# Weight products that stream their columns from last to first

## The chip, the cores and the metric
One NeuronCore of one Trainium2 chip. The metric is device time in microseconds (us) of one execution; the kernel before takes 2789.39 us, the median of three runs (2787.94 to 2789.61).

## The reference
Two transformer blocks over 256 positions of width 2048, in float32. The first block is a mixer (pooling and a gated delta rule), cross attention over a memory of 256 positions, and a gated feed-forward with a convolution of three taps. The second has a modulation computed from a vector, an attention with several branches, and a feed-forward with squared ReLU. Most of the work is products of 256 rows with large weight matrices:

```
h @ w_in   [2048, 5136]        h @ w_gate, h @ w_up   [2048, 5632]
y @ w_mix_out [2048, 2048]     f @ w_down             [5632, 2048]
h @ w_xq, mem_h @ w_xkv, o @ w_xo                     2048 x (2048, 4096, 2048)
second block: w_in_2 [2048, 5656], w_o_2 [2048, 2048], w_up_2 [2048, 8192], w_down_2 [8192, 2048]
```

## The kernel before
Every weight product is a `Phase`: n iterations over nb column blocks of `width` columns (512, in the first product 428, in the phase w_in2a 432), each block over `units` units of four K-tiles of 128 rows. Weights are float32 and the products are made with three matmuls each in the type float32r: the activations are split into a high and a low part beforehand (hhi and hlo, bhi and blo, fhi and flo, mhi and mlo, f2hi and f2lo), and the weights on the way. For each product of a K-tile, a column block and a half of the positions (128 of the 256, `h`), TensorE adds high x high, high x low and low x high into the same PSUM bank.

A unit's path is this. SyncE issues a transfer of 1 MB (856 or 864 KB in the narrow phases) from HBM into one of four `raw` slots (L817). ScalarE rounds two K-tiles at a time to float32r into `whi` (L1468), VectorE subtracts that from the raw values into `wlo` (L1960). `whi` and `wlo` are rings of four tiles of 128 x 2 x 512. TensorE waits on `unit_used` for a pair of tiles, runs twelve matmuls over it (two K-tiles, two halves, three parts; L1006 to L1008) and increments `mm_done`, for which ScalarE waits before it overwrites that place of the ring. A `raw` slot is free for the next transfer when VectorE has read it.

The weights are the moving operand (128 x width), the activations the stationary one (128 x 128). The result of a block lies in the PSUM tile `GP`, four banks of 512 float32 columns: banks 0 and 1 for the even block, 2 and 3 for the odd one. When the last K-tile has been added, ScalarE or VectorE reads the bank in the ordinary order. `last_units` (L965 to L979) holds the same three matmuls (L975 to L977) for the last two units of the last block of the last product, sorted by half. Between the products TensorE also transposes activations (L959) and computes the small matrices of the attention parts; these are plain float32 matmuls and transposes that the change does not touch (L401, L1149, L1153, L1375, L1425 among them).

The order of the work on each engine is written out by hand, and semaphores tie the engines together.

Of the kernel before, what the change touches and what calls it, by code (L numbers as in the profile page):

```python
# [31 lines left out]
UK = 4  # L32
# [114 lines left out]
def program(nc, A, out):  # L147
    PH = plan()
    order = list(PH.values())
    with ExitStack() as ctx:  # L150
        sems = {}

        def S(name):
            if name not in sems:
                sems[name] = ctx.enter_context(nc.semaphore(name))
            return sems[name]
# [8 lines left out]
        whi = [nc.alloc_sbuf_tensor_at(f"whi{i}", [P, 2, 512], F32R, offset=ring0 + 4096 * i) for i in range(NRING)]  # L165
        wlo = [nc.alloc_sbuf_tensor_at(f"wlo{i}", [P, 2, 512], F32R, offset=ring0 + 4096 * (NRING + i)) for i in range(NRING)]
# [49 lines left out]
        GP = ctx.enter_context(nc.psum_tensor("GP", [P, 4, 512], F32))  # L216
# [740 lines left out]
        def _(pe):  # L957
# [3 lines left out]
            def product(q, ahi, alo, ready, mid=None, end=None, first=None, points={}, halves=None):  # L961

                def last_units(it, b):  # L965
                    for h in range(NH):
                        t = slice(h * P, h * P + P)
                        o = GP[:, 2 * b + h, 0:q.width]
                        for u in (q.units - 2, q.units - 1):
                            for s in range(2):  # L970
                                pe.wait_ge(S("unit_used"), it * (2 * len(q.seq)) + 2 * (q.unit0 + q.seq.index(("g", b, u))) + s + 1 + CREDIT)
                                r = (q.rank[b, u] * 2 + s) % NRING
                                for k in range(2):
                                    kt = u * UK + 2 * s + k
                                    pe.matmul(o, ahi[:, kt, t], whi[r][:, k, 0:q.width], start=False, stop=False)  # L975
                                    pe.matmul(o, ahi[:, kt, t], wlo[r][:, k, 0:q.width], start=False, stop=False)
                                    m = pe.matmul(o, alo[:, kt, t], whi[r][:, k, 0:q.width], start=False, stop=(kt == q.units * UK - 1))  # L977
                                if h:
                                    m.then_inc(S("mm_done"), 1)  # L979
                        if h == 0:  # L980
                            m.then_inc(S("half_mm"), 1)

                def iteration(it, late):
                    for b, u in q.rank:
                        if q.name == "down23" and isinstance(it, int) and it == q.n - 1 and b == q.nb - 1 and u >= q.units - 2:
                            if u == q.units - 1:
                                last_units(it, b)
                            continue
                        if u == 0:
                            pe.wait_ge(S(f"evac{b % 2}"), it * (q.nb // 2) + (q.ev0 + b // 2 + 1))  # L990
                        if b == 0 and not halves:
                            pe.wait_ge(*ready(u))
                        for s in range(2):
                            if b == 0 and halves:
                                pe.wait_ge(*halves(u, s))
                            pos = q.seq.index(("g", b, u))

                            pe.wait_ge(S("unit_used"), it * (2 * len(q.seq)) + 2 * (q.unit0 + pos) + s + 1 + CREDIT)
                            r = (q.rank[b, u] * 2 + s) % NRING
                            for k in range(2):  # L1000
                                kt = u * UK + 2 * s + k
                                first, last = kt == 0, kt == q.units * UK - 1
                                for h in range(NH):
                                    t = slice(h * P, h * P + P)
                                    o = GP[:, 2 * (b % 2) + h, 0:q.width]
                                    pe.matmul(o, ahi[:, kt, t], whi[r][:, k, 0:q.width], start=first, stop=False)  # L1006
                                    pe.matmul(o, ahi[:, kt, t], wlo[r][:, k, 0:q.width], start=False, stop=False)  # L1007
                                    m = pe.matmul(o, alo[:, kt, t], whi[r][:, k, 0:q.width], start=False, stop=last)  # L1008
                            m.then_inc(S("mm_done"), 1)
                        if mid and b % 2 == 1 and u == 1:  # L1010
                            mid(it)
                        if late and b == 0 and u == 0:
                            late()
                        if (b, u) in points:
                            points[b, u]()
                        if isinstance(it, int) and (it, b, u) in points:
                            points[it, b, u]()
                    if q.ada:

                        pe.wait_ge(S("unit_used"), it * (2 * len(q.seq)) + 2 * (q.unit0 + len(q.seq)) + CREDIT)  # L1020
                        pe.wait_ge(S("ada_read"), it + (q.ada0 + 1))
                        if q.name == "ffn1a":
                            pe.wait_ge(S("f1_f"), it + 1)
                        for j in range(4):
                            m = turn(TB[:, 512 + j * P:512 + (j + 1) * P], ada_acc[:, j * P:(j + 1) * P])
                        m.then_inc(S("ada_sum"), 1)

                if end or first:
                    iteration(0, first)
                    if q.n > 1:  # L1030
                        with loop(pe, q.n - 1) as i:
                            iteration(i + 1, (lambda: end(i)) if end else None)
                    return (lambda: end(q.n - 1)) if end else None
                with loop(pe, q.n) as it:
                    iteration(it, None)
# [23 lines left out]
            def unit_of(v):  # L1059
                return v // 8, v % 8 // 4, v % 4  # L1060
# [76 lines left out]
            for hf in range(NH):  # L1137
                for j, m_ in enumerate(("upto", "after", "chunk0", "chunk1")):
                    m = pe.matmul(GP[:, 0, 32 * hf + 8 * j:32 * hf + 8 * j + 8], C(m_), gdec[:, hf * 8:hf * 8 + 8], start=True, stop=True)
                m.then_inc(S("dn_sum"), 1)  # L1140
            for hf in range(NH):
# [6 lines left out]
                for b in range(2):  # L1148
                    pe.matmul(B8[:, 4 * b:4 * b + 4, :].rearrange("p a b -> p (a b)"), C("ones"),  # L1149
                              KB[:, 4 * b:4 * b + 4, :].rearrange("p a b -> p (a b)"),  # L1150
                              start=True, stop=False, skip_group_check=True)
                    for h in range(4 * b, 4 * b + 4):
                        m = pe.matmul(B8[:, h, :], KB[:, h, :], C("negones"), start=False, stop=(h % 4 == 3),  # L1153
                                      skip_group_check=True)
                m.then_inc(S("dn_diff"), 1)
            for hf in range(NH):
                pe.wait_ge(*((S("dn_ex"), 2) if hf else (S("cv_e"), 6)))
                pe.wait_ge(S("dn_kb"), hf + 1)
                for h in range(8):
                    m = turn(AB[hf][0][:, h, :], hd(hf, 1)[:, h, :])  # L1160
                m.then_inc(S("dn_t"), 1)
            for hf in range(NH):
                pe.wait_ge(S("dn_dm"), hf + 1)
                for h in range(8):
                    m = turn(AB[hf][1][:, h, :], DN[hf]["KB"][:, h, :])
                m.then_inc(S("dn_t"), 1)
            for hf in range(NH):
                pe.wait_ge(S("dn_tc"), hf + 1)
                pe.wait_ge(S("dn_qn"), hf + 1)
                for h in range(8):  # L1170
                    m = turn(AB[hf][0][:, h, :], hd(hf, 0)[:, h, :])
                m.then_inc(S("dn_t"), 1)
            for hf in range(NH):
                pe.wait_ge(S("dn_tc"), hf + 3)
                for h in range(8):
                    m = pe.matmul(AB[hf][1][:, h, :], DN[hf]["KT"][:, h, :], DN[hf]["KBT"][:, h, :], start=True, stop=True)
                m.then_inc(S("dn_lt_mm"), 1)
            for hf in range(NH):
                pe.wait_ge(S("dn_tc"), hf + 5)
                for h in range(8):  # L1180
                    m = pe.matmul(AB[hf][0][:, h, :], DN[hf]["KT"][:, h, :], DN[hf]["QT"][:, h, :], start=True, stop=True)
                m.then_inc(S("dn_at_mm"), 1)
            for hf in range(NH):
                pe.wait_ge(S("dn_lt"), hf + 1)
                pe.wait_ge(S("dn_qd"), hf + 1)
                for h in range(8):
                    m = turn(AB[hf][1][:, h, :], hd(hf, 0)[:, h, :])
                m.then_inc(S("dn_t"), 1)
            for hf in range(NH):
                pe.wait_ge(S("dn_tc"), hf + 7)  # L1190
                for e in range(2):
                    pe.wait_ge(S("lv_m"), 2 * hf + e + 1)
                    for h in range(4 * e, 4 * e + 4):
                        m = turn(AB[hf][1][:, h, :], DN[hf]["MT"][:, h, :])
# [29 lines left out]
            for hf in range(NH):  # L1224
# [3 lines left out]
                for h in range(8):  # L1228
                    m = pe.matmul(AB[hf][0][:, h, :], DN[hf]["AA"][:, h, :], hd(hf, 2)[:, h, :], start=True, stop=True)
                m.then_inc(S("dn_uu"), 1)  # L1230
                for h in range(8):
                    m = pe.matmul(AB[hf][1][:, h, :], DN[hf]["KB"][:, h, :], DN[hf]["AA"][:, h, :], start=True, stop=True)
                m.then_inc(S("dn_uw"), 1)
            pe.wait_ge(S("dn_kd"), 2)
            for n in range(4):
                hf, c = divmod(n, 2)
                r = slice(64 * c, 64 * c + 64)
# [6 lines left out]
                if n:  # L1244
                    for e in range(2):
                        pe.wait_ge(S(f"sc_u{e}"), n)
                        for h in range(4 * e, 4 * e + 4):
                            m = pe.matmul(both[:, h, :], WQ[:, h, :], ST[:, h, :], start=(h % 4 == 0), stop=False, skip_group_check=True)
                        m.then_inc(S(f"sc_w{e}"), 1)
                for e in range(2):  # L1250
                    if n:
                        pe.wait_ge(S(f"sc_v{e}"), n)
                    if n < 3:
                        if n == 1 and e == 0:
                            pe.wait_ge(S("dn_oc"), 1)
                        for h in range(4 * e, 4 * e + 4):
                            m = pe.matmul(other[:, h, :], k3[r, h, :], V[r, h, :], start=True, stop=True)
                        m.then_inc(S(f"sc_s{e}"), 1)
                for h in range(8):
                    m = pe.matmul(both[r2, h, :], DT[r, h, r], V[r, h, :], start=(n == 0), stop=True, skip_group_check=True)  # L1260
                m.then_inc(S("sc_o"), 1)

            def dn_turn():
                for hf in range(NH):
# [3 lines left out]
                    for h in range(8):  # L1268
# [6 lines left out]
                    first=lambda: None, points={(0, 0, 1): dn_turn} | {((6 + k) // 8, *list(PH["mix_out"].rank)[(6 + k) % 8]): lambda k=k: raw_turn(1, k)  # L1275
                                                                       for k in range(8)})
            product(PH["xkva"], mhi, mlo, lambda u: (S("norm_lo"), 8 + 2 * u + 2))
            product(PH["xkvb"], mhi, mlo, lambda u: (S("norm_lo"), 16),
                    first=lambda: None, points={unit_of(2 * k): lambda k=k: raw_turn(2, k) for k in range(8)})
# [10 lines left out]
            def query_turn(g):  # L1290
# [7 lines left out]
                for f in range(4):  # L1298
# [6 lines left out]
                    first=lambda: pe.wait_ge(S("norm_lo"), 24), points={unit_of(k): lambda k=k: key_turn(k) for k in range(4)} |  # L1305
# [1232 lines left out]
```

## Time and profile before

| | |
|---|---|
| median of three runs | 2789.39 us |
| profiled execution, first to last instruction (span) | 2785.1 us |
| time around the span (median less span) | 4.3 us |
| TensorE matmuls under way | 2725.2 us, 98%, 13302 instructions |
| TensorE weight loads | 2329.5 us, 84% |
| VectorE busy | 1772.1 us, 64% |
| ScalarE busy | 1324.0 us, 48% |
| GpSimd busy | 169.5 us, 6% |
| moved by DMA | 579.60 MB, mean 208 GB/s |

The profile gives the span of the profiled execution and no time outside it, so what lies around the span is taken from the median. A matmul's duration runs from its start to the end of its pipeline, and several overlap; the distance from one start to the next tells how much of the engine one takes. Idle time of an engine is put down to the instruction that released it.

### The profile page before, as it was taken

Reading aid. Unit: us, or ns where it says so; the run is one execution under the profiler, and the core shown is the slowest. Engines: PE = TensorE matmul, PEld = TensorE weight load, DVE = VectorE, ACT = ScalarE, POOL = GpSimd, SP = SyncE. Lnnn points to the kernel's source line nnn. Section 1 sums busy time; section 2 is a strip of 40 time slices with the busy share of each in tenths; the row PEclk is TensorE's granted clock in tenths of the full one; section 3 lists DMA queues with packets and bytes.
Section 4 is the critical chain, followed back from the end, with each engine's and each line's share of the span. In section 5 each row is a group of like instructions: output and inputs, shape, how many; then the busy total and the mean of one; then the engine's idle time right before and its main releaser. Section 6 shows DMA issues by size and latency. Waiting matters only on the chain.

```text
span 2785.1 us, 34787 instructions
## 1 busy us (share of the span) xinstructions
PE 2725.2 (98%) x13302; PEld 2329.5 (84%) x13302; DVE 1772.1 (64%) x2025; ACT 1324.0 (48%) x1679; POOL 169.5 (6%) x132
## 2 busy tenths in 40 slices
PE   8999999999999999999999999998989999999998
PEld 8999988888888888888888799887868888888887
DVE  4477488776578888765555564547775756645455
ACT  5555444454445454434455454446455344344443
POOL 0001620000000000000000002720000000000000
PEclk9999999999999999999999999999999999999999
DMA  8554068887477777775555556640755866755553
GB/s 284 164 170 131 1 242 275 290 278 261 164 259 273 273 279 272 274 257 182 194 182 200 181 188 204 200 151 1 259 180 197 280 204 238 261 189 177 191 185 132
DMA packets 293266, 579.60 MB, mean 208 GB/s; under 512 B 9168, under 2 KB 46192, under 8 KB 292112
## 3 DMA queue, kind: packets, MB, share of 16 engines
q1 hardware_dynamic: 291296, 566.08, 60.4%
q0 software_dynamic: 1120, 8.57, 0.8%
q10 hardware_dynamic: 720, 3.15, 0.3%
q8 instruction: 90, 1.47, 0.2%
q14 instruction: 40, 0.33, 0.0%
HBM read 575.66 MB, written 2.10 MB: 207 GB/s over the span
## 4 chain that ended last, share of the span: by engine, by line
PE 95%; DVE 3%; ACT 1%; issue 1%; DMA 0%; SPq 0%; POOL 0%; DVEq 0%; ACTq 0%
PE GP L1006 28%; PE GP L1008 28%; PE GP L1007 28%; PE TA L959 2%; PE TB L959 2%; PE TB L607 1%; PE TB L426 1%; PE GP L401 0%; PE TA L1375 0%; DVE wlo L1960 0%; PE GP L1216 0%; PE TA L1216 0%; PE GP L1203 0%; DMA x<-in_x 0%; DVE x L2402 0%
## 5 line engine op out<-in xcount | busy, mean ns | idle before, releaser
L1960 DVE TENSOR_TENSOR wlo<-raw,whi 128x1024 fp32r<-128x1024 f32 (+2 forms) x904 | 1088.2, 1217 | 812.2 <-ACT whi L1468 803.2
L1468 ACT CAST whi<-raw 128x1024 fp32r<-128x1024 f32 (+2 forms) x904 | 923.7, 1029 | 1170.8 <-PE GP L1008 1109.5
L1006 PE MATMUL GP<-whi,hhi 128*128 128x512 f32 (+2 forms) x1792 | 689.9, 385 | 1.9 <-issue 1.4
L1008 PE MATMUL GP<-whi,hlo 128*128 128x512 f32 (+2 forms) x1792 | 681.6, 380 | 0.0
L1007 PE MATMUL GP<-wlo,hhi 128*128 128x512 f32 (+2 forms) x1792 | 680.8, 380 | 0.0
L1006 PEld LDWEIGHTS GP<-whi,hhi 128*128 128x128 f32 x1792 | 338.1, 189 | 52.2 <-issue 3.3
L1008 PEld LDWEIGHTS GP<-whi,hlo 128*128 128x128 f32 x1792 | 337.8, 188 | 52.0
L1007 PEld LDWEIGHTS GP<-wlo,hhi 128*128 128x128 f32 x1792 | 338.3, 189 | 50.5 <-issue 1.0
L1006 PE MATMUL GP<-whi,bhi 128*128 128x512 f32 x704 | 277.0, 393 | 0.2 <-DVE blo L2021 0.2
L1948 DVE SCALAR_TENSOR_TENSOR ada_acc<-raw,csig,ada_acc 128x512 f32<-128x512 f32 x360 | 270.3, 751 | 10.2
L1008 PE MATMUL GP<-whi,blo 128*128 128x512 f32 x704 | 274.6, 390 | 0.0
L1007 PE MATMUL GP<-wlo,bhi 128*128 128x512 f32 x704 | 274.3, 390 | 0.0
L1006 PE MATMUL GP<-whi,f2hi 128*128 128x512 f32 x496 | 195.4, 394 | 0.0
L1008 PE MATMUL GP<-whi,f2lo 128*128 128x512 f32 x496 | 193.3, 390 | 0.0
L1007 PE MATMUL GP<-wlo,f2hi 128*128 128x512 f32 x496 | 193.3, 390 | 0.0
L1008 PEld LDWEIGHTS GP<-whi,blo 128*128 128x128 f32 x704 | 132.2, 188 | 27.8
L1006 PEld LDWEIGHTS GP<-whi,bhi 128*128 128x128 f32 x704 | 132.3, 188 | 26.9 <-DVE blo L2021 0.7
L1007 PEld LDWEIGHTS GP<-wlo,bhi 128*128 128x128 f32 x704 | 132.4, 188 | 26.5
L1006 PE MATMUL GP<-whi,fhi 128*128 128x512 f32 x352 | 137.5, 391 | 0.0
L1008 PE MATMUL GP<-whi,flo 128*128 128x512 f32 x352 | 137.2, 390 | 0.0
L1007 PE MATMUL GP<-wlo,fhi 128*128 128x512 f32 x352 | 137.1, 390 | 0.0
L1007 PEld LDWEIGHTS GP<-wlo,f2hi 128*128 128x128 f32 x496 | 93.2, 188 | 20.0 <-issue 1.0
(437 smaller groups left out, 2578.2 us busy)
## 6 DMA issues: line engine op xcount, KB each, us to landing
raw<-in_w_up SPq DMA_DIRECT2D x108, 1024.0 KB, 5.4
raw<-in_w_down SPq DMA_DIRECT2D x108, 1024.0 KB, 5.1
raw<-in_w_ada SPq DMA_DIRECT2D x96, 1024.0 KB, 5.2
raw<-in_w_gate SPq DMA_DIRECT2D x44, 1024.0 KB, 5.3
raw<-in_w_in SPq DMA_DIRECT2D x48, 856.0 KB, 4.7
raw<-in_w_xkv SPq DMA_DIRECT2D x32, 1024.0 KB, 5.7
raw<-in_w_in SPq DMA_DIRECT2D x24, 1024.0 KB, 5.0
raw<-in_w_in SPq DMA_DIRECT2D x24, 864.0 KB, 4.7
```

The lines of the kernel that those rows point to most:

```text
L426: m = pe.matmul(TB[:, 512 * (n % 2) + d * P:512 * (n % 2) + d * P + P], kv[:, k, c:c + P], pT[:, k, j, :], start=(k == 0), stop=(k == 1), ...
L607: m = pe.matmul(bank[:, j * P:j * P + P], l, r, start=(d == 0), stop=(d == len(terms) - 1), skip_group_check=True)
L959: return pe.transpose(dst, src, ident[0:n, 0:n] if n != P else ident)
L1006: pe.matmul(o, ahi[:, kt, t], whi[r][:, k, 0:q.width], start=first, stop=False)
L1007: pe.matmul(o, ahi[:, kt, t], wlo[r][:, k, 0:q.width], start=False, stop=False)
L1008: m = pe.matmul(o, alo[:, kt, t], whi[r][:, k, 0:q.width], start=False, stop=last)
L1468: nc.scalar.copy(whi[(2 * g + s) % NRING][:, :, 0:q.width], raw[j % NSLOT][:, 2 * s:2 * s + 2, 0:q.width])\
L1948: m = nc.vector.scalar_tensor_tensor(ada_acc[:, :], raw[j % NSLOT][:, k, :], c, ada_acc[:, :], ALU.mult, ALU.add)
L1960: TTo(wlo[r][:, :, 0:q.width], raw[j % NSLOT][:, 2 * s:2 * s + 2, 0:q.width], whi[r][:, :, 0:q.width].bitcast(F32), ALU.subtract).then_inc ...
```

## The change
In both places where weight products are issued, the moving operand and the output are indexed with `[:, ::-1]` on the column dimension. The moving operand is read from column width-1 down to 0, and the result of its first column is written to the last PSUM column, and so on down. The stationary operand, the contents of all tiles, the flags and all waits and increments stay. Column j of the weights still ends in column j of PSUM.

```diff
@@ last_units
-                        o = GP[:, 2 * b + h, 0:q.width]
+                        o = GP[:, 2 * b + h, 0:q.width][:, ::-1]
...
-                                    pe.matmul(o, ahi[:, kt, t], whi[r][:, k, 0:q.width], start=False, stop=False)
-                                    pe.matmul(o, ahi[:, kt, t], wlo[r][:, k, 0:q.width], start=False, stop=False)
-                                    m = pe.matmul(o, alo[:, kt, t], whi[r][:, k, 0:q.width], start=False, stop=(kt == q.units * UK - 1))
+                                    pe.matmul(o, ahi[:, kt, t], whi[r][:, k, 0:q.width][:, ::-1], start=False, stop=False)
+                                    pe.matmul(o, ahi[:, kt, t], wlo[r][:, k, 0:q.width][:, ::-1], start=False, stop=False)
+                                    m = pe.matmul(o, alo[:, kt, t], whi[r][:, k, 0:q.width][:, ::-1], start=False, stop=(kt == q.units * UK - 1))
@@ iteration
-                                    o = GP[:, 2 * (b % 2) + h, 0:q.width]
-                                    pe.matmul(o, ahi[:, kt, t], whi[r][:, k, 0:q.width], start=first, stop=False)
-                                    pe.matmul(o, ahi[:, kt, t], wlo[r][:, k, 0:q.width], start=False, stop=False)
-                                    m = pe.matmul(o, alo[:, kt, t], whi[r][:, k, 0:q.width], start=False, stop=last)
+                                    o = GP[:, 2 * (b % 2) + h, 0:q.width][:, ::-1]
+                                    pe.matmul(o, ahi[:, kt, t], whi[r][:, k, 0:q.width][:, ::-1], start=first, stop=False)
+                                    pe.matmul(o, ahi[:, kt, t], wlo[r][:, k, 0:q.width][:, ::-1], start=False, stop=False)
+                                    m = pe.matmul(o, alo[:, kt, t], whi[r][:, k, 0:q.width][:, ::-1], start=False, stop=last)
```

## Rows read from the trace of the kernel before

**Rows 1.** The page: engine busy times, and TensorE's granted clock in 40 slices.
```profile
PE 2725.2 (98%) x13302; PEld 2329.5 (84%) x13302; DVE 1772.1 (64%) x2025; ACT 1324.0 (48%) x1679; POOL 169.5 (6%) x132
...
PEclk9999999999999999999999999999999999999999
```

**Rows 2.** The page: the chain that ended last, by engine and by line.
```profile
PE 95%; DVE 3%; ACT 1%; issue 1%; DMA 0%; SPq 0%; POOL 0%; DVEq 0%; ACTq 0%
PE GP L1006 28%; PE GP L1008 28%; PE GP L1007 28%; PE TA L959 2%; PE TB L959 2%; PE TB L607 1%; PE TB L426 1%; PE GP L401 0%; PE TA L1375 0%; DVE wlo L1960 0%; PE GP L1216 0%; PE TA L1216 0%; PE GP L1203 0%; DMA x<-in_x 0%; DVE x L2402 0%
```

**Rows 3.** Waits, longest first: total us, times, longest (all; TensorE's; the transfer queue's).
```profile
ACT whi L1468 <- PE GP L1008: 1109.5, 755, 3.6
DVE wlo L1960 <- ACT whi L1468: 803.2, 607, 4.5
...
PE TA L959 <- DVE xn_p L2303: 11.3, 1, 11.3
...
PE GP L1006 <- DVE wlo L1960: 0.5, 1, 0.5
...
SPq L817 <- DVE wlo L1960: 2097.6, 448, 110.1
```

**Rows 4.** Groups by line and shape, matmuls of L1006 and L975: busy, mean ns | idle.
```profile
L1006 PE MATMUL GP<-whi,hhi 128*128 128x512 f32 x1216 | 481.5, 396 | 1.9 <-issue 1.4 <-DVE wlo L1960 0.5
L1006 PE MATMUL GP<-whi,bhi 128*128 128x512 f32 x704 | 277.0, 393 | 0.2 <-DVE blo L2021 0.2
L1006 PE MATMUL GP<-whi,f2hi 128*128 128x512 f32 x496 | 195.4, 394 | 0.0
L1006 PE MATMUL GP<-whi,hhi 128*128 128x428 f32 x384 | 139.4, 363 | 0.0
L1006 PE MATMUL GP<-whi,fhi 128*128 128x512 f32 x352 | 137.5, 391 | 0.0
L1006 PE MATMUL GP<-whi,mhi 128*128 128x512 f32 x256 | 100.9, 394 | 0.0
L1006 PE MATMUL GP<-whi,hhi 128*128 128x432 f32 x192 | 69.0, 359 | 0.0
L975 PE MATMUL GP<-whi,f2hi 128*128 128x512 f32 x16 | 6.2, 390 | 0.0
```

**Rows 5.** Timeline, three stretches: start us, duration us, engine, line, operation.
```profile
102.32 0.36 PE L1006 MATMUL GP<-whi,hhi 128*128 128x428 f32 x1
102.33 0.19 PEld L1007 LDWEIGHTS GP<-wlo,hhi 128*128 128x128 f32 x1
...
103.50 0.36 PE L1006 MATMUL GP<-whi,hhi 128*128 128x428 f32 x1
...
1500.17 0.39 PE L1007 MATMUL GP<-wlo,fhi 128*128 128x512 f32 x1
...
1505.61 0.39 PE L1007 MATMUL GP<-wlo,fhi 128*128 128x512 f32 x1
...
1689.72 0.36 PE L1006 MATMUL GP<-whi,hhi 128*128 128x432 f32 x1
...
1692.65 0.36 PE L1006 MATMUL GP<-whi,hhi 128*128 128x432 f32 x1
```

**Rows 6.** The chain in order of time (first row), then single lines: durations min/median/max.
```profile
731.76 6.92 PE GP L401 x32
...
L1149 PE MATMUL TB<-flat,cst x4: 593/594/677, 262.4 to 264.6; 128*128 128x512 f32 x4
L1425 PE MATMUL TA<-dg,cst x16: 590/592/697, 1960.2 to 2537.5; 128*128 128x512 f32 x16
L1153 PE MATMUL TB<-cst,flat x16: 272/275/276, 263.3 to 265.8; 128*128 128x128 f32 x16
L1375 PE MATMUL TA<-rc,w1c x128: 191/275/276, 1756.4 to 1831.4; 128*128 128x31 f32 x128
```

## The prediction

> **What bounds the kernel now.** I read the page first: TensorE has matmuls under way in 98% of the span and its granted clock is 9 tenths or more, the upper of its two levels (2.4 GHz), in every one of 40 slices [rows 1]. Busy time of a pipelined engine can mislead, so the chain of waits comes next: of the work that ended last 95% is TensorE's, and the three matmul lines that the change edits, L1006 to L1008, hold 28% each [rows 2]. Third are the waits. ScalarE waited 1109.5 us for L1008 and VectorE waited 803.2 us for ScalarE, that is, the two engines that prepare weight tiles are ahead and stand behind TensorE's release of a ring tile; the transfer queue waited 2097.6 us for VectorE in turn. TensorE's own longest wait is 11.3 us, and for the prepared weights it waited 0.5 us in all [rows 3]. So the pace at which TensorE streams one weight matmul sets the time, and whatever that pace gains or loses is the change's whole effect.
>
> **How many, and how far apart.** Grouped by shape, line 1006 has 1216 + 704 + 496 + 352 + 256 matmuls of 512 columns, 384 of 428 and 192 of 432; L975 has 16 more of 512 columns [rows 4]. L1007 and L1008 (and L976, L977) run once for each of these, so 3 x 3040 = 9120 matmuls have 512 columns, 1152 have 428, 576 have 432; 10848 are touched.
> The mean durations (390 to 396 ns) are not their price, as matmuls overlap. Their spacing is: from 1500.17 to 1505.61 us lie 24 starts, 226.7 ns each, at 512 columns; from 102.32 to 103.50 lie 6, 196.7 ns each, at 428; from 1689.72 to 1692.65 lie 15, 195.3 ns each, at 432 [rows 5]. The sum 9120 x 0.2267 + 1152 x 0.1967 + 576 x 0.1953 = 2067.5 + 226.6 + 112.5 = 2406.6 us is 86% of the span of 2785.1 us, against some 85% in the chain, so the spacing is the right price.
> At 2.4 GHz 512 columns take 213.3 ns at one a cycle. The stream therefore already runs at one column a cycle, with a gap of 13.4 ns per matmul. The narrow ones have 178.3 and 180.0 ns of columns in a spacing 16 to 18 ns longer; their weight loads last 0.19 us [rows 5] and probably hold them, so that a small cost to the narrow matmuls may be partly covered.
>
> **The change part by part.** It adds no instruction, no wait, no byte and no transfer. Tiles, tile order, the semaphores and the ring are untouched. No queue is passed and nothing moves past a wait. Where a matmul writes, only the order within its own bank row changes, and every consumer waits for the whole matmul. Two orders turn round.
> 1. The moving operand is read from its last column to its first. Step is one element (4 bytes) back in place of one forward. All 512 are still neighbours.
> 2. The PSUM columns are written last to first. The consumers read the bank as before.
> No row of the trace has a matmul with a backward operand, so the price has to be bounded. From below: the 13.4 ns gap goes altogether, 9120 x 13.4 ns = 122 us; nothing excludes it, though nothing in the order of columns suggests it. From above: the nearest rows of a slower stream are the plain float32 matmuls. 32 of L401 with 256 columns take 6.92 us, 216 ns each, which is 0.845 ns or two cycles a column [rows 6]; and at equal shape, 128x512, L1149 and L1425 last 594 and 592 ns against 390 ns of the edited lines [rows 4, 6], 203 ns more. If a backward column cost two cycles, spacings would be 432, 361 and 365 ns, so 9120 x 0.206 + 1152 x 0.165 + 576 x 0.170 = 1879 + 190 + 98 = +2167 us.
> I take nothing, zero, of this range for either order. The reason is locality: the backward stream touches the same words of the same row, and words that were neighbours in time still are; only the sign of the step differs. The row that it is nearest to is the same matmul forward, same bytes and same tiles, rather than the float32 matmul, whose operands are another type. Same engine, same clock: L1375's moving slices of 31 floats start at odd offsets for every other l [rows 6] and show a median of 275 ns, no different from the 275 ns of L1153 with 128 aligned columns; but both look bound by the weight load, so this is weak support.
> What would hide a cost: nothing. With the preparers waiting for TensorE [rows 3], each nanosecond on a matmul is 10.8 us on the kernel. What comes late next if TensorE slows: nobody, the others only wait longer. ScalarE's and VectorE's exposure does not change, as PSUM is read in the old order in the other banks.
> A rule of the Trainium skill speaks against the change. Its page "PSUM — Partial Sum Buffer" (Specifications) has PSUM in lines of 8 bytes, two float32 values, and says that any non-contiguous access pattern slows matmuls significantly; the page "SBUF — State Buffer" (section "SBUF: two separate sides") has 16-byte lines in SBUF that give full rate when a line is hit at least twice in a row. No row here has a non-contiguous operand at this width, so neither is tested by the trace. Read as a rule on the step's sign, the first would give the two-cycle rival below; read as a rule on lines, both give nothing: widths 512, 428 and 432 are even and start at column 0, so backward neighbours still share their lines. I hold the second reading the likelier.
>
> **The sum.** 2785.1 us of span + 4.3 us around it (median 2789.4 less the span) + 0 = 2789.4 us, the median of the runs shown.
>
> **Rivals.**
> A, slower by far: one of the two address streams pairs neighbours only when the address rises, and falls to one column each two cycles. Its place is every edited matmul, its price the +2167 us above: 2789 + 2167 = 4956 us. It decides as soon as a column takes more than one cycle. For it: two cycles a column is a pace that this engine shows on other operands [rows 6], and the forward stream runs so near the ceiling that it has no reserve. Against it: neighbours stay neighbours. If a column took more than two cycles it would be above that.
> B, slower a little: a fixed cost at the head of a backward matmul, such as a first fetch that is no longer ready. It spans from the visible 0.5 ns per matmul (5.6 us) to a second gap of 13.4 ns, 9120 x 13.4 = 122 us and 0 to 23 us for the 1728 narrow ones: 2795 to 2935 us, 2861 with half a gap. For it: there is a 13.4 ns gap now, so heads of matmuls are not free. Against it: the addresses are known well ahead of the matmul.
> C, faster: the gap comes from writes of one matmul meeting the next one's at the same end of the bank and the backward order eases it: down to 2667 us with the whole gap. Against it: both matmuls turn round, so their distance in the bank stays what it was.
> D, the reversal of both sides is folded away before it reaches the chip, or the engine treats both signs alike: the time is that of the forecast, and I count it there.
>
> **Chances.** Forecast and D 0.68, A 0.18, B 0.11, C 0.03. A measurement of this kernel can tell some 0.2% (5.6 us) from no change; so faster 0.03, same 0.68, slower 0.29. The range goes from 2783 (0.2% below) to 2936 us, which takes in the forecast, all of B and a little of C, 0.8 in sum, and leaves A out; the forecast's own range is 2784 to 2795.
>
> **What will show it.** Right: start-to-start spacing of L1006 to L1008 at 512 columns stays at 226 to 227 ns, their durations at 390 ns, ScalarE's wait for L1008 at about 1110 us. A shows as a spacing above 400 ns, durations near 590 ns, a ScalarE wait above 3000 us, DMA at half its rate. B shows as the same added nanoseconds on 512 columns whatever the tile, and fewer on 428 and 432. Wrong altogether would be a spacing that differs between L1007 and L1008, whose operands lie in different tiles: then it is the place of data and not the order.

## The result and the profile after

The kernel takes 2844.14 us, the median of four runs (2842.31 to 2846.10), against 2788.66 us before (2786.57 to 2789.61). The ratio is 1.020, 95% interval 1.0187 to 1.0213: slower by 55.5 us. The forecast was no change (2789.4 us). The time lies inside the stated range, in the part that rival B held (2795 to 2935 us). The profiled execution took 2844.97 us, of which 2843.1 us is span.

The page of the kernel after: engine busy times, the granted clock in 40 slices, the chain of waits by engine.
```profile
PE 2785.1 (98%) x13302; PEld 2329.2 (82%) x13302; DVE 1777.2 (63%) x2025; ACT 1323.1 (47%) x1679; POOL 167.7 (6%) x132
...
PEclk9999999999999999999999999999999999999999
...
PE 96%; DVE 2%; ACT 1%; issue 1%; DMA 0%; SPq 0%; POOL 0%; DVEq 0%; ACTq 0%
```
The clock and the kind of bound are as in [rows 1, 2]. TensorE's busy time rose by 59.9 us; the busy times of weight loads, VectorE and ScalarE moved by 5.1 us at most.

Waits of the kernel after, in the columns of [rows 3].
```profile
ACT whi L1468 <- PE GP L1008: 1170.8, 761, 3.6
...
DVE wlo L1960 <- ACT whi L1468: 851.8, 613, 4.7
...
PE TA L959 <- DVE xn_p L2303: 11.3, 1, 11.3
```
No new wait has come. ScalarE stands 61 us longer behind TensorE and VectorE 49 us longer behind ScalarE; that is the delay passed on, not a cause.

The cause is seen in the spacing. Timeline of TensorE after, three stretches as in [rows 5].
```profile
103.32 0.36 PE L1006 MATMUL GP<-whi,hhi 128*128 128x428 f32 x1
...
105.68 0.36 PE L1006 MATMUL GP<-whi,hhi 128*128 128x428 f32 x1
...
1529.72 0.40 PE L1007 MATMUL GP<-wlo,fhi 128*128 128x512 f32 x1
...
1535.32 0.40 PE L1007 MATMUL GP<-wlo,fhi 128*128 128x512 f32 x1
...
1719.87 0.36 PE L1006 MATMUL GP<-whi,hhi 128*128 128x432 f32 x1
...
1723.42 0.36 PE L1006 MATMUL GP<-whi,hhi 128*128 128x432 f32 x1
```
At 512 columns 24 starts take 5.60 us, 233.3 ns each, where it was 226.7 ns: +6.7 ns. At 428 columns 12 starts take 2.36 us, 196.7 ns each, and at 432 columns 18 starts take 3.55 us, 197.2 ns each. Set beside [rows 5], 428 columns seem not to have moved, but the six starts there are too few: printed starts are rounded to 0.01 us, and before the change the spacing at 428 columns differs from stretch to stretch. Longer stretches of the kernel before:
```profile
154.85 0.36 PE L1007 MATMUL GP<-wlo,hhi 128*128 128x428 f32 x1
...
168.38 0.36 PE L1008 MATMUL GP<-whi,hlo 128*128 128x428 f32 x1
...
1615.30 0.36 PE L1007 MATMUL GP<-wlo,hhi 128*128 128x432 f32 x1
...
1723.02 0.36 PE L1008 MATMUL GP<-whi,hlo 128*128 128x432 f32 x1
```
and the same ones after:
```profile
156.87 0.36 PE L1007 MATMUL GP<-wlo,hhi 128*128 128x428 f32 x1
...
170.63 0.37 PE L1008 MATMUL GP<-whi,hlo 128*128 128x428 f32 x1
...
1648.44 0.36 PE L1007 MATMUL GP<-wlo,hhi 128*128 128x432 f32 x1
...
1756.97 0.36 PE L1008 MATMUL GP<-whi,hlo 128*128 128x432 f32 x1
```
The 70 starts at 428 columns take 13.53 us before and 13.76 us after, 193.3 and 196.6 ns each; the 550 starts at 432 columns 107.72 and 108.53 us, 195.9 and 197.3 ns each.

The mean over the whole trace gives the price. It takes every distance below 260 ns from one weight matmul to the next of the same width: 227.1 ns before and 233.4 ns after at 512 columns (+6.3), 195.1 and 196.7 ns at 428, 195.9 and 197.3 ns at 432 (+1.5 each). At 512 columns the even stretches before run at 226.7 ns, but single distances of 231 to 236 ns lie between them, which lifts that mean to 227.1. With the counts of the prediction, 9120 x 6.3 ns + 1728 x 1.5 ns = 57.5 + 2.6 = 60.1 us; the span grew by 2843.1 - 2785.1 = 58.0 us. So the sum explains the whole, and 2 us too much: the some 120 distances of 260 ns and more at 512 columns did not grow but fell by 2.0 us in all.

Groups by line and shape after, in the columns of [rows 4].
```profile
L1006 PE MATMUL GP<-whi,bhi 128*128 128x512 f32 x704 | 282.1, 401 | 0.0
L1007 PE MATMUL GP<-wlo,bhi 128*128 128x512 f32 x704 | 279.9, 398 | 0.0
L1008 PE MATMUL GP<-whi,blo 128*128 128x512 f32 x704 | 279.7, 397 | 0.0
...
L1006 PE MATMUL GP<-whi,hhi 128*128 128x428 f32 x384 | 140.9, 367 | 0.0
```
Durations are 7 to 8 ns longer at 512 columns (401 against 393 ns in the first row). It is the same for the three lines, whose moving tiles differ, so the place of the data has no part in it.

### The profile page after: what moved, and what is told of

Its sections match the earlier page's. It is cut to its first block, busy times and chain, and to the rows that moved or that the text cites. A ratio compares the mean times of both kernels' runs of the same rounds, so it can differ in the third digit from the quotient of the medians.

```text
span 2843.1 us, 34787 instructions
## 1 busy us (share of the span) xinstructions
PE 2785.1 (98%) x13302; PEld 2329.2 (82%) x13302; DVE 1777.2 (63%) x2025; ACT 1323.1 (47%) x1679; POOL 167.7 (6%) x132
## 4 chain that ended last, share of the span: by engine, by line
PE 96%; DVE 2%; ACT 1%; issue 1%; DMA 0%; SPq 0%; POOL 0%; DVEq 0%; ACTq 0%
PE GP L1006 29%; PE GP L1007 29%; PE GP L1008 29%; PE TA L959 2%; PE TB L959 2%; PE TB L607 1%; PE TB L426 1%; PE GP L401 0%; PE TA L1375 0%; PE GP L1203 0%; PE TA L1203 0%; PE GP L1216 0%; PE TA L1216 0%; DMA x<-in_x 0%; DVE wlo L1960 0%
## 5 line engine op out<-in xcount | busy, mean ns | idle before, releaser
L1006 PE MATMUL GP<-whi,hhi 128*128 128x512 f32 (+2 forms) x1792 | 699.8, 390 | 2.0 <-issue 1.4
L1007 PE MATMUL GP<-wlo,hhi 128*128 128x512 f32 (+2 forms) x1792 | 691.8, 386 | 0.0
L1008 PE MATMUL GP<-whi,hlo 128*128 128x512 f32 (+2 forms) x1792 | 691.7, 386 | 0.0
L1006 PEld LDWEIGHTS GP<-whi,hhi 128*128 128x128 f32 x1792 | 337.6, 188 | 61.4 <-issue 3.7
L1008 PEld LDWEIGHTS GP<-whi,hlo 128*128 128x128 f32 x1792 | 337.4, 188 | 60.5
L1007 PEld LDWEIGHTS GP<-wlo,hhi 128*128 128x128 f32 x1792 | 337.7, 188 | 58.1 <-issue 1.0
L1006 PE MATMUL GP<-whi,bhi 128*128 128x512 f32 x704 | 282.1, 401 | 0.0
L1007 PE MATMUL GP<-wlo,bhi 128*128 128x512 f32 x704 | 279.9, 398 | 0.0
L1008 PE MATMUL GP<-whi,blo 128*128 128x512 f32 x704 | 279.7, 397 | 0.0
L1006 PE MATMUL GP<-whi,f2hi 128*128 128x512 f32 x496 | 199.2, 402 | 0.0
L1007 PE MATMUL GP<-wlo,f2hi 128*128 128x512 f32 x496 | 197.1, 397 | 0.0
L1008 PE MATMUL GP<-whi,f2lo 128*128 128x512 f32 x496 | 197.1, 397 | 0.0
L1008 PEld LDWEIGHTS GP<-whi,blo 128*128 128x128 f32 x704 | 132.4, 188 | 31.8
L1006 PEld LDWEIGHTS GP<-whi,bhi 128*128 128x128 f32 x704 | 132.4, 188 | 31.1 <-DVE blo L2021 0.4
L1007 PEld LDWEIGHTS GP<-wlo,bhi 128*128 128x128 f32 x704 | 132.5, 188 | 30.7
L1006 PE MATMUL GP<-whi,fhi 128*128 128x512 f32 x352 | 140.2, 398 | 0.0
L1007 PE MATMUL GP<-wlo,fhi 128*128 128x512 f32 x352 | 139.9, 397 | 0.0
L1008 PE MATMUL GP<-whi,flo 128*128 128x512 f32 x352 | 139.9, 397 | 0.0
L1006 PEld LDWEIGHTS GP<-whi,f2hi 128*128 128x128 f32 x496 | 93.3, 188 | 23.0 <-issue 1.0
```

Source lines behind the costliest of these rows:

```text
L1006: pe.matmul(o, ahi[:, kt, t], whi[r][:, k, 0:q.width][:, ::-1], start=first, stop=False)
L1007: pe.matmul(o, ahi[:, kt, t], wlo[r][:, k, 0:q.width][:, ::-1], start=False, stop=False)
L1008: m = pe.matmul(o, alo[:, kt, t], whi[r][:, k, 0:q.width][:, ::-1], start=False, stop=last)
```

## The experiments

**1 and 2: one stream at a time.** Experiment 1 reverses only the moving operand, experiment 2 only the output.
```diff
# 1: the three moving operands, output as before
+ pe.matmul(o, ahi[:, kt, t], whi[r][:, k, 0:q.width][:, ::-1], ...)
# 2: the output, moving operands as before
+ o = GP[:, 2 * (b % 2) + h, 0:q.width][:, ::-1]
```
Expected of 1: 

> Only the moving operand is read backwards; PSUM is written forwards, so the columns of every weight product come out in reversed order (the computation is changed in that, its amount is not). Theory R (the backward read costs 6.7 ns per matmul of 512 columns): spacing 233.3 ns, time about 2844 us. Theory W (the backward write costs it): spacing 226.7 ns, time about 2789 us. Theory B (each stream has a share, or only the pair costs): in between, for instance 230 ns and 2817 us.

Expected of 2: 

> Only the PSUM columns are written backwards; the moving operand is read forwards, so the columns of every weight product come out in reversed order. Theory R: spacing 226.7 ns, about 2789 us. Theory W: spacing 233.3 ns, about 2844 us. Theory B: in between, about 230 ns and 2817 us.

Measured: reading backwards 2845.68 us, ratio to before 1.0208 (1.0191 to 1.0225); writing backwards 2786.83 us, ratio 0.9998 (0.9988 to 1.0008), beside 2787.59 us of the kernel before in the same session. Timeline of TensorE with the read backwards:
```profile
2305.75 0.40 PE L1008 MATMUL GP<-whi,hlo 128*128 128x512 f32 x1
...
2311.35 0.40 PE L1008 MATMUL GP<-whi,hlo 128*128 128x512 f32 x1
```
and with the write backwards:
```profile
2305.71 0.39 PE L1007 MATMUL GP<-wlo,hhi 128*128 128x512 f32 x1
...
2311.15 0.39 PE L1007 MATMUL GP<-wlo,hhi 128*128 128x512 f32 x1
```
Both pairs are 24 starts apart: 5.60 us or 233.3 ns each, and 5.44 us or 226.7 ns each. The read carries the whole cost, the write none. Over the whole trace the means at 512 columns are 233.4 ns with the read backwards and 227.1 ns with the write backwards, as after and before the change. Theory R stands, W and B fall.

**3 and 4: which part of going backwards.** Experiment 3 takes groups of four columns from last to first and goes forwards inside them; experiment 4 takes the groups forwards and goes backwards inside. Both streams have the pattern.
```diff
# 3, on the output and the three moving operands
+ whi[r][:, k, 0:q.width].rearrange("p (a b) -> p a b", b=4)[:, ::-1, :]
# 4
+ whi[r][:, k, 0:q.width].rearrange("p (a b) -> p a b", b=4)[:, :, ::-1]
```
Expected of 3: 

> Both streams go through groups of four columns (16 bytes) from the last group to the first, and forwards within a group; the result is in place. If the sign of the step across lines costs, spacing 233.3 ns as in the changed kernel. If the sign of the step from word to word costs, 226.7 ns. If the cost came per line and not per matmul, it would show here more than there: 128 groups in each matmul. A two-level pattern may have a price of its own, up to two cycles a column (above 420 ns).

Expected of 4: 

> Both streams go through the groups of four columns forwards, and through the four columns of a group backwards; the result is in place. If the sign of the word-to-word step costs, 233.3 ns or more; if the sign across lines costs, 226.7 ns. As a third way, the pattern starts at column 3 and ends at 508, so the head of the next matmul lies near the start of the row as in the kernel before: if the place of the first column costs, 226.7 ns here and 233.3 ns with groups from last to first.

Measured, one run each: 2849.07 us and 2790.65 us. Timeline of experiment 3:
```profile
2305.62 0.40 PE L1008 MATMUL GP<-whi,hlo 128*128 128x512 f32 x1
...
2311.22 0.40 PE L1008 MATMUL GP<-whi,hlo 128*128 128x512 f32 x1
```
and of experiment 4:
```profile
2305.72 0.39 PE L1007 MATMUL GP<-wlo,hhi 128*128 128x512 f32 x1
...
2311.16 0.39 PE L1007 MATMUL GP<-wlo,hhi 128*128 128x512 f32 x1
```
Again 24 starts each: 233.3 and 226.7 ns. A negative step inside 16 bytes is free, 384 of them per matmul. Going from group to group backwards costs the full 6.7 ns, and the 127 jumps cost no more than 511 single steps do. In experiment 3 both streams have the pattern, so that its cost too is the read's is inferred from experiments 1 and 2, and not shown for groups.

**5: whose cost it is.** Only the second of the three matmuls is reversed.
```diff
+ pe.matmul(o[:, ::-1], ahi[:, kt, t], wlo[r][:, k, 0:q.width][:, ::-1], start=False, stop=False)
```
Expected: 

> Only the second of the three matmuls (L1007, and L976) reads and writes backwards, the result stays in place. Theory H (a fixed cost of each backward matmul): mean spacing (2 x 226.7 + 233.3) / 3 = 228.9 ns, about 2808 us, and the trace shows which spacing is the long one: the one that begins with the start of L1007 if the backward matmul holds the stream longer, the one that ends there if its own start is late. Theory T (the cost comes at a change between matmuls, because a backward one ends at column 0 and the next backward one begins at 511, or because directions differ): all three spacings move, or none.

Measured: 2806.81 us, one run; a third of 55.5 us above before would be 2807. Groups of experiment 5:
```profile
L1007 PE MATMUL GP<-wlo,bhi 128*128 128x512 f32 x704 | 278.8, 396 | 0.0
...
L1008 PE MATMUL GP<-whi,blo 128*128 128x512 f32 x704 | 274.7, 390 | 0.0
```
Between 2230 and 2498 us, in the mean of the distances below 260 ns and from the trace's starts in whole nanoseconds, 232.5 ns lie from L1007 to the next start, 226.7 from L1006 and 227.5 from L1008. Against the 226.7 ns of an even forward stretch the reversed matmul takes 5.8 ns more and the one that follows it 0.8 more, together 6.7 ns before rounding; the one before it does not change. (From the printed starts the same means come out at 233.3, 226.8 and 226.7. Three distances take 686.7 ns here, nine take 2060, so the rounding to 0.01 us falls alike again and again and does not average out.) Nearly all of the cost lies in the distance that begins with the reversed matmul's own start. Theory H stands and T, by which all three would have moved or none, falls.

**6, 11 and 12: how coarse the jumps may be.** Groups of 256, 16 and 64 columns, last group first, forwards inside; in 11 and 12 only the products of 512 columns.
```diff
+ def groups_back(w, n=16):        # 12: n=64; 6: n = width // 2 and no condition
+     return w.rearrange("p (a b) -> p a b", b=n)[:, ::-1, :] if w.shape[1] == 512 else w
```
Expected of 6: 

> Both streams read the upper half of the columns forwards, then the lower half forwards (one jump backwards per matmul, first column 256); the result stays in place. Theory P (the place of the first column, or a single backward jump, costs 6.7 ns): 233.3 ns. Theory L (the cost belongs to stepping backwards from line to line, and 511 steps and 127 jumps of four columns reached the same limit): 226.7 ns, about 2788 us.

Expected of 11: 

> Both streams of the 512-column products go through groups of 16 columns from the last to the first, forwards inside a group; the narrow products are forward. 31 backward jumps per matmul, against 127 with groups of four (233.3 ns) and one with groups of 256 (226.7 ns). Theory count (each backward line step costs a little, up to a ceiling): between, 227 to 233 ns. Theory head (only the first few fetches count, the stall comes when they go backwards): with four lines forward at the head the stall is gone, 226.7 ns. Theory place (a start far from column 0 and near the end of the row costs): 233.3 ns.

Expected of 12: 

> The same with groups of 64 columns: 7 backward jumps, first column 448. Theory count: 226.7 to 228 ns. Theory head: 226.7 ns. Theory place: 233.3 ns, as column 448 is nearer the end of the row than 256, which cost nothing.

Measured, one run each: 2785.73 us with groups of 256, 2847.24 us with 16, 2786.44 us with 64. Timeline with groups of 16:
```profile
2305.66 0.40 PE L1010 MATMUL GP<-wlo,hhi 128*128 128x512 f32 x1
...
2311.26 0.40 PE L1010 MATMUL GP<-wlo,hhi 128*128 128x512 f32 x1
```
and with groups of 64:
```profile
2306.05 0.39 PE L1009 MATMUL GP<-whi,hhi 128*128 128x512 f32 x1
...
2311.49 0.39 PE L1009 MATMUL GP<-whi,hhi 128*128 128x512 f32 x1
```
24 starts each, 233.3 and 226.7 ns; groups of 256 give 226.7 ns too. The cost is all there or not at all: full with 511, 127 and 31 backward jumps, none with 7 and 1. The graded form of theory count falls, as does theory head as I had put it (four groups of 16 bytes at the head would have been enough). A count that tips over between 7 and 31 jumps and a head longer than 16 columns are both left open. So is a third reading that no run separates from these: the step back grows with the group, 1, 7 and 31 columns long where it costs, 127 and 511 where it does not. As in experiment 3, both streams have the pattern. Theory place is dealt with under experiment 10.

**7 and 8: is the weight load in the way?** 64 in place of 128 stationary columns, on all K-tiles but the first and last of a block; 8 reads and writes backwards as well.
```diff
+ np_ = P if first or last else 64
+ t = slice(h * P, h * P + np_)
+ o = GP[0:np_, 2 * (b % 2) + h, 0:q.width]
```
Expected of 7: 

> The kernel before, but for the K-tiles other than the first and the last of a block only 64 of 128 stationary columns are used (half of the output rows are left out there). Theory S (the gap beyond 213.3 ns is the weight load's reads standing in the way of the moving reads, so it goes with the number of stationary columns): gap halves from 13.3 to 6.7 ns, spacing 220 ns. Theory F (the gap is fixed per matmul): 226.7 ns.

Expected of 8: 

> As the kernel with 64 stationary columns, both moving read and PSUM write backwards. Theory S: the gap of 20 ns of the changed kernel halves, spacing 223.3 ns. Theory F: 233.3 ns, or 6.7 ns above the forward kernel of this kind whatever that is.

Measured, one run each: 2806.31 us forwards and 2850.98 us backwards. Groups of experiment 7, a weight load; before, its mean was 188 to 189 ns:
```profile
L1008 PEld LDWEIGHTS GP<-wlo,hhi 128*64 128x64 f32 x1568 | 211.0, 135 | 127.1 <-issue 1.3
```
Timeline of experiment 7:
```profile
2305.69 0.39 PE L1008 MATMUL GP<-wlo,hhi 128*64 128x512 f32 x1
2305.91 0.39 PE L1009 MATMUL GP<-whi,hlo 128*64 128x512 f32 x1
2306.14 0.40 PE L1007 MATMUL GP<-whi,hhi 128*64 128x512 f32 x1
2306.38 0.39 PE L1008 MATMUL GP<-wlo,hhi 128*64 128x512 f32 x1
...
2311.21 0.39 PE L1008 MATMUL GP<-wlo,hhi 128*64 128x512 f32 x1
```
and of experiment 8:
```profile
2305.62 0.40 PE L1008 MATMUL GP<-wlo,hhi 128*64 128x512 f32 x1
...
2307.72 0.40 PE L1008 MATMUL GP<-wlo,hhi 128*64 128x512 f32 x1
```
The load is shorter by 54 ns and the matmuls are no closer: 24 starts in 5.52 us, 230.0 ns, with durations of 0.39 and 0.40 us mixed. The backward twin has 9 starts in 2.10 us, 233.3 ns. Theory S fails in both. Theory F fails too for the forward kernel, whose spacing rose by 3.3 ns, which neither had foreseen; for the backward one its first form (233.3 ns) holds. The two runs also shorten the loads of the narrow products, where the means over the whole trace are 193.7 ns at 428 columns and 193.5 at 432 forwards, 196.7 and 198.2 backwards. So a load 54 ns shorter takes only 1.4 and 2.4 ns off the forward spacing there, and the backward cost shows more, 3.0 and 4.7 ns in place of 1.5.

**9 and 10: fewer columns.** 448 of 512 columns on all K-tiles but the first of a block, forwards and backwards.
```diff
+ wd = q.width if kt == 0 else min(q.width, 448)
+ o = GP[:, 2 * (b % 2) + h, 0:wd]            # 10: [:, ::-1], also on whi and wlo
```
Expected of 9: 

> The kernel before, but products of 512 columns use only the first 448 on all K-tiles but the first of a block (that part of the products is left out). It is the base for the backward twin. With 448 / 2.4 = 186.7 ns of columns and the gap of 13.3 ns: spacing 200.0 ns, unless the weight load holds it as it does the narrow products (195.3 to 196.7 ns).

Expected of 10: 

> The same with both streams backwards. Theory fixed (one stall of 6.7 ns per backward matmul): 206.7 ns, or 6.7 above the twin. Theory proportional (6.7 ns / 512 columns): 5.8 ns above the twin, 205.8 ns. Theory cover (a weight load that ends late hides the stall, as the row of the narrow products of 428 columns suggests, which did not move): less than 5 ns above the twin.

Measured, one run each: 2593.69 and 2623.39 us, 29.7 us apart. Timeline forwards:
```profile
2305.83 0.36 PE L1008 MATMUL GP<-wlo,hhi 128*128 128x448 f32 x1
...
2311.91 0.36 PE L1008 MATMUL GP<-wlo,hhi 128*128 128x448 f32 x1
```
and backwards:
```profile
2310.99 0.37 PE L1008 MATMUL GP<-wlo,hhi 128*128 128x448 f32 x1
...
2315.95 0.37 PE L1008 MATMUL GP<-wlo,hhi 128*128 128x448 f32 x1
```
Forwards 30 starts take 6.08 us, 202.7 ns each; backwards 24 take 4.96 us, 206.7 ns each. The difference is 4.0 ns, below both 6.7 and 5.8, as theory cover has it. Over the whole traces the means are 202.8 and 206.6 ns. Beyond the 186.7 ns of its columns the backward matmul has 20.0 ns in the mean, as at 512 (233.3 - 213.3), while the forward one has 16.0 where it had 13.3. The 20.0 are a mean of two values, though: about half of the backward distances at 448 columns are 202 to 204 ns and half 209 to 211, while at 512 nearly all are 233 or 234. So the spacing of fewer columns has a limit that is already there in the forward kernel and covers a part of the cost: 6.3 ns show at 512 columns, 3.8 at 448, 1.5 at 432 and 428. That this limit is a late weight load, as theory cover says, is not shown. Theory place falls as the only cause: here the first column read is 447 and the cost is there, in experiment 12 it is 448 and there is none.

## Where the prediction was right and where it was wrong

- **What bounds the kernel**: right. Time follows the spacing of the weight matmuls, with the counts 9120, 1152 and 576; a loss in the spacing is hidden by nothing, and only waits behind TensorE grew.
- **The write backwards costs nothing**: right, experiment 2, ratio 0.9988 to 1.0008. The page "PSUM — Partial Sum Buffer" of the Trainium skill (Specifications), by which any non-contiguous pattern slows matmuls significantly, does not hold for a step of -1, if that counts as one, nor for the two-level patterns of experiments 4, 6 and 12, all at 226.7 ns.
- **The read backwards costs nothing**: this is the step that failed. "I take nothing, zero, of this range for either order", argued from locality: words that were neighbours in time still are. Experiment 4 shows that locality is right within 16 bytes. It says nothing on the order of the groups, and that order costs 6.7 ns per matmul of 512 columns (experiments 1 and 3). Case D, by which both signs are treated alike, falls with it. The page "SBUF — State Buffer" of the Trainium skill (SBUF: two separate sides), which asks for two hits in a row on a 16-byte line, is met by the changed kernel and by experiments 3 and 11, and they are slow all the same: the rule is not enough to call a pattern free.
- **Rival A** (two cycles a column): false; the spacing came to 233.4 ns in the mean, not above 400. The plain float32 matmuls were the wrong neighbours to bound this one by.
- **Rival B** (a small fixed cost): this is what happened. It was priced with half a gap per matmul, and 6.7 ns is half of 13.4. That the two agree is luck: half was the middle of an interval, and nothing in the text singled it out. Its 2861 us is 17 us above the measured time. Most of this is two terms: 9 us are the narrow products, which it charged in full (1728 x 6.7 ns = 12 us) and which took 1.5 ns each (2.6 us), and some 4 us are 6.3 in place of 6.7 ns at 512 columns. Its cause was put as "at the head of a backward matmul"; that the cost is the matmul's own is shown by experiment 5, that it sits at its head is not.
- **The range**: it held the time only because it took in rival B, at a chance of 0.11. The forecast itself (2789.4 us, 0.68) missed by 55 us.
- **The narrow products are partly covered**: right, 1.5 ns at 428 and at 432 columns where 6.3 show at 512. The forward spacing of 196.7 ns at 428 columns was read from six starts, and the mean over the trace is 195.1; what 432 columns have beyond their 180.0 ns is 15.3 ns by the prediction's own figures and not 16. I had named the weight load as what holds the narrow products. Its 0.19 us lies near the spacing, but with loads of 0.13 us (experiment 7) the spacing fell by only 1.4 and 2.4 ns, so the length of the load is not what holds them; what does is open.
- **Rival C** (faster): false; with the output alone reversed the mean spacing is 227.1 ns, as before.
- **The weights of the cases.** With 10.8 us on the kernel for each nanosecond per matmul, and no row with the operand in question, 0.68 on a change below 0.5 ns was too sure. The sensitivity was in the text and not in the chances.
- **The time around the span**: 4.3 us was the median less the span. The four executions after have 1.8 to 1.9 us around their spans, so the span of 2785.1 us probably belongs to an execution of some 2787 us, faster than the median. The sum of the forecast is not touched by this.

Open: what the engine does in those 6.7 ns; whether the number of backward jumps, their length or a head of more than 16 and up to 64 columns decides; what covers the cost as the columns get fewer; and whether the stall at 512 columns would be the same for other types. A stationary operand read in another order was not tried.

## What to carry to other kernels

Where one instruction is issued ten thousand times on the path that sets the end, price "nothing changes in it" at its smallest visible unit (here 0.5 ns) before giving it two thirds of the chance. A change of a matmul's output order in PSUM was free here; if a moving float32r operand has to be read from its end, do it in blocks of 64 columns (256 bytes) or more, or reverse only within 16 bytes: at 512 columns both ran at the forward pace. Take a spacing from tens of starts, not from six, as printed starts are rounded. Split a two-sided change into its sides at once; two runs settled which side it was.

## What the runs showed of the hardware that was not expected

- Reading the moving operand backwards costs 6.7 ns per matmul of 512 columns in an even stretch, all or none: full with groups of 1, 4 and 16 columns, none with 64 and 256, none for reversal inside four (groups of 4 and more were tried with both streams at once). With fewer columns less of it shows: 3.8 ns at 448, 1.5 ns at 432 and 428, in the mean.
- Fewer stationary columns (64 for 128) shortened the weight load from 188 to 135 ns and made the forward stream slower, 230.0 against 226.7 ns; the whole kernel took 2806.31 us with less work.
- The forward stream carries 13.7 ns per matmul beyond its columns at 512 (13.3 in an even stretch), 16.1 at 448, 15.9 at 432 and 16.8 at 428, in the mean over the trace. That a shorter weight load does not shrink it at 512 columns speaks against the load's length as its cause; experiment 7 also halves the output rows, and these two are not separated.
